# Another order of a body's steps in a hybrid attention and recurrent layer: both recurrent-input projections first, scores and gates one projection sooner

## What is computed

```python
h = rmsnorm(x, ln_gain)                              # 2048 x 1024
q, k, v, g_attn, x_lru, g_lru = split(h @ w_in)      # 1024 + 256 + 256 + 1024 + 1024 + 1024 columns
q, k = partial_rope(q), partial_rope(k)              # first 16 of 64 dimensions
y_attn = sliding_window_attention(q, k, v, sinks)    # 16 heads, 4 kv heads, window 128, blocks of 128
y_attn = rmsnorm(y_attn * silu(g_attn), attn_out_gain)
u = causal_depthwise_conv(x_lru, conv_w, conv_b)     # width 4
r, i = sigmoid(u @ w_rgate + b_r), sigmoid(u @ w_igate + b_i)   # 16 blocks of 64
a = exp(-8 * r * softplus(-lambda))
h_t = a_t * h_(t-1) + sqrt(1 - a_t**2) * i_t * u_t   # scan over positions
y_lru = rmsnorm(h_t * silu(g_lru), lru_out_gain)
out = rmsnorm(x + concat(y_attn, y_lru) @ w_out, final_gain)
```

## Time and profile before

| what | before |
|---|---|
| median of 3 runs | 1423.26 us (1422.80 to 1424.64) |
| the profiled execution: its time | 1424.16 us |
| its span, first to last instruction | 1422.6 us |
| TensorE clock granted, mean | 0.997 of full speed |
| DMA traffic | 243.27 MB, 171 GB/s |
| first XL0 matmul of body 0 / last of the bodies' | 42.62 / 1007.17 us |
| weight subtraction on VectorE (L1006), 33 of them | 1.22 us each |
| VectorE's longest waits in body 1 | 1.30 us for Square (L896), 0.82 for `cu` (L862), 0.42 for `p_hi` (L846) |
| scan on VectorE (L1287), 32 | 2.27 us mean |

### The profile page before, as it was taken

How to read it: one execution, slowest core, us unless ns; L and a number is a source line. 1 busy time by engine, 2 the same in 40 slices (tenths; PEclk the granted TensorE clock), 3 DMA queues, 4 the chain that set the end, 5 groups by cost and what they waited for, 6 DMA issues and landing times.

```text
span 1422.6 us, 21721 instructions
## 1 busy us (share of the span) xinstructions
PE 1377.9 (97%) x6464; PEld 1134.5 (80%) x6464; DVE 1008.3 (71%) x1725; ACT 765.3 (54%) x1551; POOL 314.1 (22%) x316
## 2 busy tenths in 40 slices
PE   5999999999999999999999999999999999999998
PEld 4778777888888887888888888788877888888886
DVE  4798989987777878787787877787886644344442
ACT  5677686756566574757566574657565322222120
POOL 2131413232231414232231413232230000000000
PEclk9999999999999999999999999999999999999999
DMA  8767676763636364554636374554717333232320
GB/s 218 252 241 245 244 236 234 258 199 146 225 119 222 140 215 150 186 185 146 222 128 230 127 276 144 186 173 170 224 50 248 118 89 116 61 118 86 91 89 30
DMA packets 151872, 243.27 MB, mean 171 GB/s; under 512 B 35456, under 2 KB 101248, under 8 KB 151808
## 3 DMA queue, kind: packets, MB, share of 16 engines
q1 hardware_dynamic: 144784, 217.86, 45.6%
q0 software_dynamic: 7024, 24.65, 5.2%
HBM read 179.55 MB, written 62.91 MB: 170 GB/s over the span
## 4 chain that ended last, share of the span: by engine, by line
PE 45%; DVE 21%; issue 18%; ACT 9%; POOL 3%; SPq 1%; DMA 1%; DVEq 1%; ACTq 1%; POOLq 0%
PE ring L1414 20%; PE acc_b L201 12%; PE ring L201 11%; DVE hs L1287 5%; POOL ri L622 2%; DVE p_lo L1224 2%; ACT p_sb L838 2%; DVE s_sb L1198 2%; PE ps_v L1464 2%; DVE cu L1253 1%; DVE smax L1211 1%; DVE o_sb L1233 1%; ACT cu L862 1%; ACT kc_ol L851 1%; DVE ya L1184 1%
## 5 line engine op out<-in xcount | busy, mean ns | idle before, releaser
L1414 PE MATMUL ring<-split,w_hi 128*128 128x512 f32 x2304 | 719.1, 393 | 7.8 <-DVE split L1026 7.2
L1414 PEld LDWEIGHTS ring<-split,w_hi 128*128 128x128 f32 x2304 | 427.1, 189 | 94.9 <-DVE split L1026 8.0
L1414 PE MATMUL ring<-split,w_lo 128*128 128x512 f32 x1152 | 450.4, 391 | 0.0
L1414 PEld LDWEIGHTS ring<-split,w_lo 128*128 128x128 f32 x1152 | 216.8, 188 | 46.6
L838 ACT ACTIVATE p_sb<-s_sb,smax 128x129 f32<-128x129 f32 x256 | 99.9, 393 | 118.7 <-DVE smax L1211 118.5
L622 POOL TENSOR_TENSOR ri<-ri,hs 128x512 f32<-128x512 f32 x32 | 53.9, 1704 | 383.0 <-ACT hs L904 383.0
L1253 DVE SCALAR_TENSOR_TENSOR cu<-xl,prm,cu 128x512 f32<-128x512 f32 x96 | 72.2, 752 | 43.0 <-ACT cu L862 34.0
L778 ACT ACTIVATE q_st<-qrot 64x512 fp32r<-64x512 f32 x64 | 40.4, 631 | 114.9 <-DVE qrot L1089 114.1
L201 PE MATMUL acc_b<-wo_rest,y_own 128*128 128x512 f32 x384 | 89.9, 390 | 2.9 <-DVE wo_rest L162 2.3
L201 PE MATMUL ring<-split,y_own 128*128 128x512 f32 x384 | 91.3, 392 | 0.1
L1685 ACT ACTIVATE w_hi<-res 128x1024 fp32r<-128x1024 f32 x15 | 15.9, 1060 | 134.3 <-DVE res L1755 134.3
(11 more groups left out here) (203 smaller groups left out, 2478.0 us busy)
## 6 DMA issues: line engine op xcount, KB each, us to landing
w_hi<-w_split_scratch SPq DMA_DIRECT2D x108, 512.0 KB, 3.2
w_lo<-w_split_scratch SPq DMA_DIRECT2D x108, 512.0 KB, 4.3
w_split_scratch<-w_hi SPq DMA_DIRECT2D x36, 512.0 KB, 5.1
w_split_scratch<-w_lo SPq DMA_DIRECT2D x36, 512.0 KB, 5.7
w_raw<-w_in_d SPq DMA_DIRECT2D x32, 512.0 KB, 4.4
...
```

The source lines that it names most:

```text
L1414: last = mm(bank(r), w[:, i % WSLOTS, k, :], h[:, par, k, :], start=(k == 0 and j == 0), stop=(k == KC - 1 and j == 2))
```

## The change

The functions compute what they did. `softmax_a` is cut into `select` and `top`, `gather_o` into `add_o` and `gate_o`, `lru_mid` into `one_less` and `input_x`, and `decays` into `take_r`, `take_i` and `decays`; the bodies of all five engines call them in another order, and ring and weight slots follow. The diff, with its indentation reduced and the declarations of the cut functions shortened:

```diff
-XL0, GL0, XL1, GA0, GA1, GL1, KVG, Q0, Q1 = range(9)
+XL0, XL1, GL0, GA0, GA1, GL1, KVG, Q0, Q1 = range(9)
-(R_XL0, R_GL0, R_XL1, R_R0, R_I0, R_GA0, R_R1, R_I1, R_GA1, R_XT0, R_XT1, R_GL1, R_KV, R_Q0, R_Q1,
+(R_XL0, R_XL1, R_R0, R_I0, R_GL0, R_R1, R_I1, R_GA0, R_GA1, R_XT0, R_XT1, R_GL1, R_KV, R_Q0, R_Q1,
 R_VT) = range(16)
...
     load(XL0, COL_XL)
-    load(GL0, COL_GL)
+    load(XL1, COL_XL + P)
         sp.dma_start(xb, x[0, bass.ds((g + (q + 1) * KV) * P, P), :]).then_inc(*x_in.one())
-    load(XL1, COL_XL + P)
     sp.wait_ge(*gw_low.at(n, 0))
     for j, w in enumerate((w_rgate, w_igate)):
+    load(GL0, COL_GL)
...
 def body(n, g, par, q, following, nxt_par, split, split_next, last):
+    p_current(n, 0)
     lru_tail(n, 0)
     lru_tail(n, 1)
+    p_current(n, 1)
     lru_gate(n, 0)
-    p_current(n, 0)
-    p_current(n, 1)
+    p_current(n, 2)
     if not last:
         if nxt_par != par:
             pool.wait_ge(table_in, (q + 2) * 32)
         sine_k(n)
-    p_current(n, 2)
+    p_current(n, 3)
     lru_gate(n, 1)
     if not last:
         sine_q(n, 0)
-    p_current(n, 3)
-    if not last:
         sine_q(n, 1)
     write_out(n, g, q)
...
-    def decays(u):
...
+
+    def take_i(u):
+        G = g * UNITS + u
+        act.wait_ge(*ring_ready.at(n, (R_I0, R_I1)[u] + 1))
+        act.sem_inc(settled, 1)
+        nc.scalar.activation(ri[u][:, :], bank((R_I0, R_I1)[u]), ACT.Tanh, scale=0.5,
+                             bias=prm[:, G, C_BI:C_BI + 1]).then_inc(*ring_act.one())
+
+    def decays(u):
+        G = g * UNITS + u
+        act.wait_ge(*decay.at(n, 3 * u + 1))
         nc.scalar.activation(ra[u][:, :], ra[u][:, :], ACT.Exp, scale=prm[:, G, C_NEG4SP:C_NEG4SP + 1],
                              bias=prm[:, G, C_NEG4SP:C_NEG4SP + 1]).then_inc(*decay.one())
...
         nc.scalar.activation(a2[:, :], ra[u][:, :], ACT.Square).then_inc(*decay.one())
-        act.wait_ge(*ring_ready.at(n, (R_I0, R_I1)[u] + 1))
-        act.sem_inc(settled, 1)
-        nc.scalar.activation(ri[u][:, :], bank((R_I0, R_I1)[u]), ACT.Tanh, scale=0.5,
-                             bias=prm[:, G, C_BI:C_BI + 1]).then_inc(*ring_act.one())
...
-    if split:
-        split_w(n, GA0)
-    high_u(0)
-    gate_l(0)
-    if split:
-        split_w(n, GA1)
     if q < NQUART - 1:
         act.wait_ge(*one_minus.at(n, 0))
         square_x(n, x_in.at(n, 1), x_sq, x_norm.at(n, 0))
...
         proj.high_y(act, 0, 0)
     elif g > 1:
         proj.high_w(act, 2 * g - 4)
-        proj.high_w(act, 2 * g - 3)
+    high_u(0)
+    if split:
+        split_w(n, GA0)
     lru_in(1)
     s_copy(0)
+    take_r(0)
+    high_u(1)
+    take_i(0)
+    if split:
+        split_w(n, GA1)
+    s_exp(0)
+    gate_l(0)
     decays(0)
-    high_u(1)
+    s_copy(1)
+    take_r(1)
+    decays(1)
+    s_exp(1)
     if split:
         split_w(n, GL1)
-    s_exp(0)
+    high_p(0)
+    s_copy(2)
+    take_i(1)
     gate_a(0)
-    decays(1)
-    s_copy(1)
     if q < NQUART - 1:
         root_x(n, x_ms.at(n, 1), x_root)
     lru_root(0)
     lru_root(1)
     if split_next:
         split_w(n, KVG)
-    s_exp(1)
+    s_exp(2)
     gate_a(1)
-    high_p(0)
-    s_copy(2)
+    high_p(1)
+    low_o(0)
+    s_copy(3)
     if q < NQUART - 1:
         for half in range(2):
             high_x(h_hi[:, 1 - par], g * P, half, bank(R_XT0 + half),
                    ring_ready.at(n, R_XT0 + half + 1), h_high.one())
+    elif g > 1:
+        proj.high_w(act, 2 * g - 3)
     if last:
         act.wait_ge(*ring_ready.at(n, R_GA1 + 1))
         proj.high_y(act, 0, 1)
+    s_exp(3)
     if split_next:
         split_w(n, Q0)
-    s_exp(2)
+    high_p(2)
+    low_o(1)
     gate_l(1)
-    low_o(0)
-    high_p(1)
-    s_copy(3)
     if last:
         act.wait_ge(*ring_ready.at(n, R_GL1 + 1))
...
         proj.high_w(act, 5)
     if split_next:
         split_w(n, Q1)
-    s_exp(3)
     if not last:
         take_kv(n)
-    low_o(1)
-    high_p(2)
+    low_o(2)
+    high_p(3)
     if split_next:
         split_w(n, NG + XL0)
-    if not last:
-        take_q(n, 0)
-        high_k(n)
-    low_o(2)
-    high_p(3)
     if last:
         proj.high_w(act, 6)
+    if not last:
+        high_k(n)
+        take_q(n, 0)
+    low_o(3)
+    if split_next:
+        split_w(n, NG + XL1)
+    if not last:
+        high_q(n, 0)
+        take_q(n, 1)
+        take_v(n)
+        high_v(n)
     if split_next:
         split_w(n, NG + GL0)
     if not last:
-        high_q(n, 0)
-        take_q(n, 1)
-    low_o(3)
-    if not last:
-        take_v(n)
-    if split_next:
-        split_w(n, NG + XL1)
-    if not last:
         high_q(n, 1)
-        high_v(n)
...
-    def softmax_a(b):
...
                                   ).then_inc(*s_sel.one())
+
+    def top(b):
+        s = s_sb[:, b % 2, :, 0:BLK]
...
-    def gather_o(b):
...
+
+    def gate_o(b):
         dve.wait_ge(*o_sum.at(n, 2 * b + 2))
...
-    def lru_mid(u):
...
+
+    def input_x(u):
         dve.wait_ge(*ring_act.at(n, FREED_BY_ACT.index((R_I0, R_I1)[u]) + 1))
...
     low_u(0)
-    if split:
-        split_w(n, GA0)
-    silu_l(0)
     if q < NQUART - 1:
         stat_x(x_sq.at(n, 1), x_ms)
+    elif g == 1:
+        proj.low_y(dve, 0, 0)
     elif g > 1:
         proj.low_w(dve, 2 * g - 4)
     conv(1)
-    softmax_a(0)
+    select(0)
     low_u(1)
     if split:
+        split_w(n, GA0)
+    top(0)
+    softmax_b(0)
+    silu_l(0)
+    if split:
         split_w(n, GA1)
-    lru_mid(0)
-    softmax_b(0)
-    silu_a(0)
-    lru_mid(1)
+    one_less(0)
+    input_x(0)
+    select(1)
+    top(1)
+    one_less(1)
+    softmax_b(1)
     if split:
         split_w(n, GL1)
+    low_p(0)
+    select(2)
+    top(2)
+    input_x(1)
+    silu_a(0)
+    if q < NQUART - 1:
         norm_x(n, x_root.at(n, 1), x_rs, x_norm)
-    softmax_a(1)
-    if q < NQUART - 1:
-        if not split:
-            norm_x(n, x_root.at(n, 1), x_rs, x_norm)
-    elif g == 1:
-        proj.low_y(dve, 0, 0)
-    elif g > 1:
-        proj.low_w(dve, 2 * g - 3)
     lru_scan(0)
     if split_next:
         split_w(n, KVG)
-    lru_scan(1)
-    low_p(0)
-    softmax_b(1)
+    softmax_b(2)
+    low_p(1)
+    add_o(0)
     silu_a(1)
-    softmax_a(2)
+    select(3)
+    top(3)
     if q < NQUART - 1:
         for half in range(2):
             low_x(h_lo[:, 1 - par], h_hi[:, 1 - par], g * P, half, bank(R_XT0 + half),
                   h_high.at(n, half + 1), ring_dve.one())
+    elif g > 1:
+        proj.low_w(dve, 2 * g - 3)
+    gate_o(0)
+    lru_scan(1)
     if split_next:
         split_w(n, Q0)
-    softmax_b(2)
-    gather_o(0)
-    low_p(1)
-    softmax_a(3)
-    if split_next:
-        split_w(n, Q1)
+    low_p(2)
+    add_o(1)
+    softmax_b(3)
+    gate_o(1)
     silu_l(1)
     if last:
         proj.low_y(dve, 0, 1)
-    softmax_b(3)
+        proj.low_w(dve, 4)
+    if split_next:
+        split_w(n, Q1)
     if not last:
         if nxt_par != par:
             dve.wait_ge(table_in, (q + 2) * 32)
         turn_k(n, following)
-    low_p(2)
-    gather_o(1)
+    low_p(3)
+    add_o(2)
+    gate_o(2)
     if last:
-        proj.low_w(dve, 4)
+        proj.low_w(dve, 5)
     if not last:
         add_k(n)
     if split_next:
         split_w(n, NG + XL0)
     if not last:
+        low_k(n, following)
         turn_q(n, 0)
-    low_p(3)
-    gather_o(2)
     if last:
-        proj.low_w(dve, 5)
+        proj.low_w(dve, 6)
+    add_o(3)
+    gate_o(3)
+    if split_next:
+        split_w(n, NG + XL1)
     if not last:
-        low_k(n, following)
         add_q(n, 0)
+        low_q(n, 0)
+        previous_v(n, following)
+        turn_q(n, 1)
+        differ_v(n)
+        low_v(n, following)
     if split_next:
         split_w(n, NG + GL0)
     if not last:
-        low_q(n, 0)
-        turn_q(n, 1)
-        previous_v(n, following)
-    if last:
-        proj.low_w(dve, 6)
-    gather_o(3)
-    if not last:
-        differ_v(n)
         add_q(n, 1)
-    if split_next:
-        split_w(n, NG + XL1)
-    if not last:
         low_q(n, 1)
-        low_v(n, following)
...
     project(n, XL0, par, split)
-    project(n, GL0, par, split)
     project(n, XL1, par, split)
     score(0)
     gates(0)
-    project(n, GA0, par, split)
+    project(n, GL0, par, split)
     gates(1)
     score(1)
-    project(n, GA1, par, split)
+    project(n, GA0, par, split)
     turn_p(0)
     score(2)
+    project(n, GA1, par, split)
+    weigh_v(0)
+    turn_p(1)
+    score(3)
     if q < NQUART - 1:
         turn_x()
     project(n, GL1, par, split, q < NQUART - 1)
-    weigh_v(0)
-    turn_p(1)
-    score(3)
+    weigh_v(1)
+    turn_p(2)
     if nxt_par != par:
         pe.wait_ge(*ring_dve.at(n, FREED_BY_DVE.index(R_XT1) + 1))
     if not last:
...
     else:
         pe.wait_ge(*ring_dve.at(n, FREED_BY_DVE.index(R_GA1) + 1))
+        pe.wait_ge(*ring_act.at(n, FREED_BY_ACT.index(R_R1) + 1))
         pe.wait_ge(*signals_b.y_low.at(0, 1))
         for e in range(3):
```

(21 more changed lines are left out.)

11 lines of the change are left out of this document (7 added, 4 removed).

## The result

The changed kernel takes **1435.66 us** (median of 4 runs, 1435.23 to 1436.47) beside 1423.95 for the kernel before on the same chip: ratio 1.0082, 95% interval 1.0064 to 1.0099. It is slower by 0.8%. The profiled execution took 1435.58 us with a span of 1433.9.

What follows compares the result with a forecast made beforehand. TensorE was taken to bound middle bodies (floor 62.7 us), VectorE's loop the first quarter. Terms -0.9 + 13.8 + 1.6 + 2 - 1 + 5.5 - 1 = +20 gave 1444, hence 1443 us at the median; range 1420 to 1457.

Steps and rivals of the forecast that it cites:

- the first rival: Whole kernel: the forecast case, slower, 1433 to 1453 us; chance 0.60.
- The middle bodies: Middle bodies: VectorE's 26.7 us chain brings gates(0) at 13.0, asked at 11.9; 1.3 charged on 62.7, so 64.0 against 63.8.
- A link: Chain from KVG to the next gates(0) on VectorE: gw_lo, between convolution and u_lo, counted as 0.7 us.
- What the change wins: TensorE: waits for the attention or weight chain go behind more matmuls, 1.0 us a body, 1.4 more in the first quarter.
- the 0.54 and the 0.46: TensorE losses in a middle body before: 0.54 us at weigh_v(0), 0.46 from projection Q1 to weigh_v(3), summed to 1.0.
- The first quarter: Bodies n = 0 to 2: 65.6 us plus 4.6 on VectorE's loop gives 70.2 each; +13.8 in all (4 to 19).
- the bare round trip: First quarter, VectorE: top(0) and softmax_b(0) become neighbours, leaving the row maximum to reciprocal wait bare, +1.9 us.
- scan(1) alone: First quarter, VectorE: scan(1) no longer beside a GpSimd multiply, 1.07 us instead of 2.36, -1.2.
- the 1.9 of both: First quarter, VectorE: norm_x comes up just as GpSimd starts its two root multiplies, +1.9 us.
- 4 to 6: Sign of being right: gates(0)'s u_hi matmul waits 4 to 6 us for u_lo in bodies 0 to 3.
- The end: Last body: GL0's projection now lies behind gates(0), +5.5 us; p_lo and subtraction waits fall by about 1.
- The rule of the second case: Middle tail: VectorE let in between GpSimd's instructions, chain 1.4 us shorter, bodies at the floor, 1429; case's chance 0.17.

Runs made afterwards that it cites:

- e2: Changed kernel with GpSimd's gate multiply of unit 1 held back by one added wait until K's add on VectorE is done; 1419.59 us, 0.9957.
- e4: Changed kernel with the edits of e1 and e2, k_lo waiting only for the first half of k_hi, and low_v cut in two; 1414.23 us, 0.9923.
- c1: Kernel before with b2's edit and the gate multiply held until K's add, then score(0) and gates(0) moved ahead of XL1's projection; 1465.0 us, 1.0291.
- e1: Changed kernel with gw_lo made behind low_u(0) and waited for only ahead of its first matmul in gates(0); 1436.62 us, 1.0078.
- b2: Kernel before with block 0's p_lo between the scans, p_hi ahead of the gate's tanh, selects ahead of the gate multiply; 1409.57 us, 0.9889.
- a1: Changed kernel with low_p(0) back behind scan(0) and GpSimd's two root multiplies ahead of block 0's selects; 1530.9 us (one execution).
- e5: e4 with the first quarter's four weight subtractions also moved into VectorE's bare round trips; 1411.43 us, 0.9906.

## Why the prediction was right, and where its steps were off

Forecast 1443 us, 1420 to 1457, slower with 0.80; measured 1435.66. The case that came is the first rival, the forecast: the middle bodies give back at `gates(0)` what they win, the first quarter loses, the last quarter gains a little. Point by point:

- **The middle bodies, right in mechanism and size.** I placed `gates(0)` 13.0 us into the body and a body at 64.0; it stands at 13.43, and bodies take 64.0. The change is shown to win its 1.0 (a body without late pieces takes 62.53, not 62.7, so it is 1.3) and to lose it at `gates(0)`: e2 and e4 remove the loss by shortening the chain, c1 makes the same wait in the other kernel. A link was misnamed: `gw_lo` costs nothing, since it lies in the shade of the `u_hi` round trip of the same length (e1).
- **"What the change wins" was not the order of groups.** I ascribed the 1.0 us to "placed by the durations above, those waits go", with TensorE's longer distance and the early p_lo in one breath. b2 wins all of it with block 0's p_lo, p_hi and selects alone, in the old order, and keeps the cover. It also shows that the 0.54 and the 0.46 were not two losses to be undone apart, as my sum had them. a1 shows that the new order needs that part just to stay near.
- **The first quarter, right as a sum, 2.2 too high against before, wrong in parts.** Bodies 69.9, 70.3, 69.4 for 70.2. The difference to before was +11.6, not +13.8: 1.2 of it because I had 65.6 for each body of before, and the distance from body 0 to 1 is 66.85; 1.0 from the bodies themselves. Of the terms, the bare round trip (1.89) and scan(1) alone (1.28 for 2.31 in this quarter) came about as counted. These did not, in the changed kernel's body 2:

```profile
222.20 3.53 POOL L622 TENSOR_TENSOR ri<-ri,hs 128x512 f32<-128x512 f32 x2 [1.48 <-ACT hs L910]
```

```profile
222.72 1.86 DVE L1030 SCALAR_TENSOR_TENSOR rows<-rows,x_stat 128x1024 f32<-128x1024 f32 x1
224.51 2.31 DVE L1303 TENSOR_TENSOR_SCAN hs<-ra,h_carry,ri 128x512 f32<-128x512 f32 x1
...
234.44 1.28 DVE L1303 TENSOR_TENSOR_SCAN hs<-ra,h_carry,ri 128x512 f32<-128x512 f32 x1
```

  norm_x got in between GpSimd's two root multiplies and lost 0.6 us (1.86 for the 1.29 it took alone in the kernel before), not the 1.9 of both; in exchange scan(0) met the second multiply and took 2.31, more than its 2.05 of before, where I had taken 1.0 off. Two things I did not have at all: `score(0)` waits for `low_q` (1.2 to 1.6 us in four bodies), so that `gates(0)` waits for only 3.3 to 3.6 where I had written 4 to 6; and the granted clock falls, which e5 (below) shows to cost such a body little. That the sum came within 1 us of 70.2 is thus in part luck: errors of both signs met.
- **The end, the step that failed.** I wrote "GL0's 5.5 us paid at the last body, +5.5; p_lo and subtraction waits of the last body fall by about 1 (0 to 2.5)", that is +4.5. From `gates(0)` of the last body to the same group of sum-of-squares matmuls of phase B, in the stretches of the kernel before:

```profile
1024.56:1109.94 85.38, 79.86 (x366) 64.08 (x365) 63.34 (x93) 51.99 (x89) 14.34 (x15) 1.00 0.46 148
```

  and of the changed kernel:

```profile
1036.31:1121.28 84.97, 83.54 (x389) 69.23 (x390) 63.98 (x96) 53.86 (x91) 12.85 (x15) 1.00 0.50 162
```

  The second stretch holds GL0's matmuls more, and is 0.4 us shorter. TensorE's idle time in it fell from 5.5 to 1.4. The waits stood in the trace of before, 5.4 us in seven rows of that stretch; in the changed kernel two of the seven are left, with 1.4. Three of those that are gone:

```profile
1054.54 0.50 PE L1464 MATMUL ps_v<-p_hi,v_hl 128*128 128x512 f32 x1 [0.74 <-DVE p_lo L1224]
1058.92 1.16 PE L201 MATMUL ring<-split,w_hi 128*128 128x512 f32 x4 [1.25 <-DVE w_lo L173]
...
1078.03 1.65 PE L201 MATMUL acc_b<-wo_rest,y_own 128*128 128x512 f32 x6 [0.63 <-DVE rms L1740]
```

  The term should have been +5.5 - 5.9. That is 4.9 of the 8.6 us by which the sum was too high; 2.2 are the first quarter's, the rest is under 1 a term. What took the waits away is not shown. A projection more behind `gates(0)` does not do it alone: c1 has one too (XL1), keeps the waits for `w_lo` (1.3) and `rms` (0.6), and pays 6.6 us for it. The changed kernel also makes the last body's `low_w` and p_lo in another order, and no run tries that part.

The rule of the second case (Trainium skill, "SBUF — State Buffer", section "SBUF: two separate sides": the pair is held "for the whole instruction") came out better than I gave it. norm_x did get in between two multiplies. The selects hold the pair as well, one at a time: K's add in e2 shows it, ending 0.54 us behind the select inside which it came up. What does not fit is `ya` in the changed kernel, which was kept out over the second select and the multiply (2.18 us), and that this depended on the multiply in the queue no row of before could show; "let in at the next boundary" remains wrong at that place.

What stays open: why a multiply that starts 0.6 us later, with the select ahead of it, wins over a VectorE operation that is there first. It was not tried with another instruction between them, and the starts that the profile gives for GpSimd are rough.
